# One attention loop instead of two: 20 steps that hold a differential and an MLA tile each, projections ahead of it, and norms computed on four columns

## The reference

```python
proj = rmsnorm(x, norm_mix) @ w_in       # 1920 columns: 15 chunks of 128
ua, cq, ckv, kr, qc, kc, vc, ud = split(proj)
ya = silu(layernorm(causal_dwconv31(glu(ua)))) @ pw + pw_b
yb = mla(rmsnorm(cq) @ w_uq, rmsnorm(ckv) @ w_ukv, rope)      # 4 heads, causal softmax
a0, a1 = softmax(q0 k0 + bias), softmax(q1 k1 + bias)         # 4 heads, two maps each
yc = rmsnorm((a0 - lam * a1) @ v)                             # "differential" attention
yd = ((windowed mean of ud) - ud) @ pool_w
x = x + concat(ya, yb, yc, yd) @ w_out
x = x + cross_attention(rmsnorm(x), rmsnorm(mem))   # its K and V: 16 chunks of mem @ wk, wv (256 tokens)
x = x + (silu(dwconv3(h @ up_g)) * dwconv3(h @ up_a)) @ down  # h = rmsnorm(x), width 2816
```

## Time and profile before

| what | value |
|---|---|
| three runs | 1738.75, 1740.1, 1740.25 us; median 1740.1 |
| the profiled execution | 1737.64 us, its span 1735.8 us |
| busy share of the span | PE 93%, PEld 71%, DVE 65%, ACT 40%, POOL 15% |
| mean granted TensorE clock | 0.975 of full speed |
| attention loop of layer 0, with the first two output chunks | 201.2 to 382.4 us |
| the same stretch of layer 1 | from 999.1 us on |

### The profile page before, as it was taken

How to read it: one execution, slowest core, us unless ns; L and a number is a source line. 1 busy time by engine, 2 the same in 40 slices (tenths; PEclk the granted TensorE clock), 3 DMA queues, 4 the chain that set the end, 5 groups by cost and what they waited for, 6 DMA issues and landing times. The chain is left out here.

```text
span 1735.8 us, 21837 instructions
## 1 busy us (share of the span) xinstructions
PE 1613.4 (93%) x7472; PEld 1239.5 (71%) x7472; DVE 1125.3 (65%) x1600; ACT 700.0 (40%) x1074; POOL 263.1 (15%) x176
## 2 busy tenths in 40 slices
PE   6889889889999999999988998899999999999996
PEld 3467576568767888888876666557867788888874
DVE  8968896664446764764765978665444674575575
ACT  3232355663344432432443244764243442342343
POOL 5513142112011000000020513212102000000002
PEclk9989999899999999999998999999999999999998
DMA  3142123223212333333224212322312232322323
GB/s 136 47 155 86 49 86 104 79 74 97 73 37 85 97 97 98 97 97 96 93 79 143 82 42 85 104 90 73 97 37 73 85 97 97 97 97 90 96 81 109
DMA packets 46205, 153.37 MB, mean 88 GB/s; under 512 B 5808, under 2 KB 6064, under 8 KB 45232
## 3 DMA queue, kind: packets, MB, share of 16 engines
q1 hardware_dynamic: 46128, 152.34, 27.5%
HBM read 144.97 MB, written 7.34 MB: 88 GB/s over the span
## 5 line engine op out<-in xcount | busy, mean ns | idle before, releaser
L688 ACT ACTIVATE wh<-raw 128x1024 fp32r<-128x1024 f32 x246 | 260.3, 1059 | 647.9 <-PE psum L1238 647.8
L1236 PE MATMUL psum<-a_hi,wh 128*128 128x512 f32 x1072 | 426.2, 398 | 12.2 <-DVE wl L927 11.8
L1237 PE MATMUL psum<-a_lo,wh 128*128 128x512 f32 x1072 | 420.4, 392 | 0.0
L1238 PE MATMUL psum<-a_hi,wl 128*128 128x512 f32 x1072 | 420.2, 392 | 0.0
L927 DVE TENSOR_TENSOR wl<-raw,wh 128x1024 fp32r<-128x1024 f32 x210 | 261.5, 1246 | 140.9 <-ACT wh L688 140.9
L1236 PE MATMUL psum<-b_hi,wh 128*128 128x512 f32 x608 | 240.2, 395 | 10.5 <-DVE wl L927 6.1
L1236 PEld LDWEIGHTS psum<-a_hi,wh 128*128 128x128 f32 x1072 | 203.1, 189 | 62.7 <-DVE wl L927 16.6
L1238 PE MATMUL psum<-b_hi,wl 128*128 128x512 f32 x608 | 236.7, 389 | 0.0
L1237 PE MATMUL psum<-b_lo,wh 128*128 128x512 f32 x608 | 236.7, 389 | 0.0
L1237 PEld LDWEIGHTS psum<-a_lo,wh 128*128 128x128 f32 x1072 | 203.2, 190 | 45.0 <-issue 2.9
L1238 PEld LDWEIGHTS psum<-a_hi,wl 128*128 128x128 f32 x1072 | 203.2, 190 | 42.7
(11 more groups left out here) (213 smaller groups left out, 2139.5 us busy)
## 6 DMA issues: line engine op xcount, KB each, us to landing
raw<-in_w_main SPq DMA_DIRECT2D x106, 512.0 KB, 3.5
raw<-in_w_up SPq DMA_DIRECT2D x88, 512.0 KB, 3.5
raw<-in_w_down SPq DMA_DIRECT2D x32, 512.0 KB, 3.5
raw<-in_w_last SPq DMA_DIRECT2D x16, 384.0 KB, 2.9
bias_scratch<-stage SPq DMA_DIRECT2D x64, 64.0 KB, 1.6
bias<-bias_scratch SPq DMA_DIRECT2D x16, 256.0 KB, 4.4
raw<-in_w_first SPq DMA_DIRECT2D x6, 512.0 KB, 3.5
sw<-in_small SPq DMA_DIRECT2D x2, 1152.0 KB, 6.7
```

Of the source, the lines that this page charges most:

```text
L688: act.activation(wh[:, b].rearrange("p k m -> p (k m)")[:, 0:width], raw[:, b, 0:width], ACT.Copy).then_inc(w_hi, 1)
L1236: pe.matmul(out_ap, wh[:, b, k, :], his[:, k, :], start=(begin and i == 0), stop=False)
L1237: pe.matmul(out_ap, wh[:, b, k, :], los[:, k, :], start=False, stop=False)
L1238: last = pe.matmul(out_ap, wl[:, b, k, :], his[:, k, :], start=False, stop=(end and i == len(tiles) - 1))
```

## The change

**Order.** Chunks 12, 13 and 14 run ahead of the loop (with the high parts of 14, 15 and 16, the exponential of lambda and the high part of the memory ahead of it on ACT as well). The loop then has 20 steps. Step t holds differential tile t (both maps), MLA tile t-1, the transposes of differential tile t-2 and MLA tile t-3, a pair of differential (even t) or MLA tiles (odd t) times values, and memory chunk t+14, whose 24 matmuls are cut in two halves of 12 with the MLA work in between. Both kinds of transposes use one bank, `TR[0]`; bank 5 becomes a third bank for the small products. The bias tiles move to other buffers and other places in SP's queue. Of the convolution's taps 43 are done ahead of the loop and 19 in steps 0 to 5 (before: 32 and 30). POOL does the high part too (`upper`) for chunks 25 to 32.

**Thin norms.** `sums_of` uses the squares as stationary operand and one column of ones as moving one, so that the sum of 128 tokens lands as one column: four columns for 512 tokens (eight for `sub`, with two heads each). ACT's root and DVE's reciprocal work on 128x4 or 128x8. `row_of` brings the result back onto all partitions: it multiplies a column, repeated as stationary operand, by the identity. For the three model norms ACT copies that row to SBUF (`row_of` on ACT). The others are read from PSUM. The last norm of the kernel (L1484 to L1502) stays as it was.

```diff
+STEPS = 20
+VX_AT = {11: 0, 13: 1, 15: 2, 17: 3}
+BIAS_AFTER = {N_WK: (0, 1, 2, 3), 19: (4,), 20: (5,), 21: (6,), 22: (7,), 23: (8,), ...
+POOL_HI = range(25, N_OUT + 2)
...
@@ sync
-                    loads_of(N_WK, 10, w_main, src_base=N_WK)
...
-                        if u in (0, 1):
-                            sp.wait_ge(acc_done, 2)
-                        elif u == 2:
-                            sp.wait_ge(v_full, V_AT["stat_kv"] + 1)
-                        elif u == 3:
-                            sp.wait_ge(g_dve, N_WK)
+                        if u == 0:
+                            sp.wait_ge(v_full, V_AT["stat_kv"] + 1)
+                        elif u == 1:
+                            sp.wait_ge(m_lo, KT)
+                        elif u == 2:
+                            sp.wait_ge(g_dve, N_WK)
+                        elif u == 3:
+                            sp.wait_ge(m_lo, KT)
...
-                    for n in range(25, 35):
+                    for n in range(N_WK, 35):
                         load(n, n % 2, w_main[layer, n])
                         for u in BIAS_AFTER.get(n, ()):
                             load_bias(u)
@@ gpsimd
+                    def upper(n):
+                        pool.wait_ge(w_load[n % 2], loads(n, n % 2))
+                        pool.wait_ge(g_full, n - 1)
+                        pool.wait_ge(w_hi, n)
+                        pool.tensor_copy(wh[:, n % 2].rearrange("p k m -> p (k m)"), raw[:, n % 2, :]).then_inc(w_hi, 1)
...
@@ scalar
+                    def roots(name, eps, scale, cols=4):
+                        act.activation(thin[:, ROOTS.index(name), 0:cols], v_wait(name)[:, 0:cols], ACT.Sqrt, bias=eps,
+                                       scale=scale).then_inc(root, 1)
+                    def row_of(name):
+                        act.activation(rbc[:], v_wait(f"{name}_row"), ACT.Copy).then_inc(v_act, 1)
...
                     for t in range(STEPS):
+                        if 2 <= t < 18:
+                            evict_pt("diff", t - 2)
                         if t < 16:
+                            exp_map("diff", t, 0)
+                            exp_map("diff", t, 1)
+                        if 3 <= t < 19:
+                            evict_pt("mla", t - 3)
+                        if 1 <= t < 17:
+                            exp_map("mla", t - 1, 0)
...
                         if n is not None:
+                            if n + 2 not in POOL_HI:
+                                hi(n + 2)
                             act.wait_ge(g_full, n + 1)
@@ vector
+                    def inverse(name, cols=4):
+                        r = ROOTS.index(name)
+                        dve.wait_ge(root, r + 1)
+                        dve.reciprocal(thin[:, r, 0:cols], thin[:, r, 0:cols]).then_inc(root_inv, 1)
...
                     for t in range(STEPS):
                         if t < 16:
...
                             for m in range(2):
+                                negatives("diff", t, m, dring[:, (2 * t + m) % 8, :], bias[t % 4], C_DIFF)
                         if 1 <= t < 17:
...
+                            inverse_sums("diff", u, slice(k, k + 2))
                             step(dve.tensor_scalar(e1, e1, rec[:, k + 1:k + 2], lam[:, 4:5], ALU.mult, ALU.mult))
                             dve.scalar_tensor_tensor(e0, e0, rec[:, k:k + 1], e1, ALU.mult,
+                                                     ALU.add).then_inc(p_ready, 1)
...
+                            negatives("mla", u, 0, ering[:, u % RING, :], mask[:, tile_at(u)[1], :], C_MLA)
+                        if 2 <= t < 18:
...
+                            dve.tensor_scalar(e, e, rec[:, u:u + 1], None, ALU.mult).then_inc(scaled_in, 1)
+                        if t < 6:
+                            convolve(4 if t == 0 else 3)
@@ tensor
+                    def sums_of(name, *pairs):
+                        ps, w = bank(name), pairs[0][1].shape[1]
+                        for j in range(4):
+                            for i, (src, one) in enumerate(pairs):
+                                last = pe.matmul(ps[:, w * j:w * j + w], src[:, P * j:P * j + P], one, start=(i == 0),
+                                                 stop=(i == len(pairs) - 1))
+                        last.then_inc(v_full, 1)
+                    def row_of(name, w=1):
+                        r = ROOTS.index(name)
+                        ps = bank(f"{name}_row")
+                        pe.wait_ge(root_inv, r + 1)
+                        for j in range(4):
+                            for i in range(w):
+                                inv = thin[:, r, w * j + i:w * j + i + 1].broadcast_to([P, P // w])
+                                last = pe.matmul(ps[P // w * i:P // w * (i + 1), P * j:P * j + P], inv, ident, ...)
+                        last.then_inc(v_full, 1)
...
                     for t in range(STEPS):
                         if t < 16:
+                            diff_scores(t)
+                        if t >= 4 and t % 2 == 0:
+                            weighted_pair("diff", t // 2 - 2)
+                        if 2 <= t < 18:
+                            turn("diff", t - 2)
+                        n = chunk_at(t)
+                        if n is not None:
+                            gemm(n, n % 2, memh, meml, M, ..., tiles=range(4), ready=ready, end=False)
+                        if 1 <= t < 17:
+                            mla_scores(t - 1)
+                        if t >= 5 and t % 2 == 1:
+                            weighted_pair("mla", t // 2 - 2)
+                        if 3 <= t < 19:
+                            turn("mla", t - 3)
...
                         if n is not None:
+                            gemm(n, n % 2, memh, meml, M, tiles=range(4, KT), ready=ready, begin=False)
```

More of the change, by code:

```diff
@@ L705, in _ @@
                     hi(1)
-                    act.activation(rtmp[:], v_wait("stat_mix"), ACT.Sqrt, bias=c("eps6"), scale=1.0 / D).then_inc(root, 1)
+                    roots("stat_mix", c("eps6"), 1.0 / D)
+                    row_of("stat_mix")
                     hi(2)
@@ L1329, in weighted_pair @@
[L1329 removed]
+                                                 ptr[:, 2 * int(kind == "diff") + place, kb, :], start=(kb == 0),
+                                                 stop=(kb == 3))
+                        last.then_inc(pv_done[kind] if qb < 3 else v_full, 1)
                     def y_ready(k):
@@ L1418, in norm_sum @@
                         pe.wait_ge(ss_in, n)
-                        product(name, (ones, ssum[:]))
+                        sums_of(name, (ssum, one))
                     gemm(N_WQ, 1, a_hi, a_lo, free="wq", ready=lambda i: pe.wait_ge(x_lo, i + 1))
                     norm_sum("stat_xa", KT)
-                    gemm(N_WQ + 1, 0, a_hi, a_lo, free="wq")
+                    gemm(N_WQ + 1, 0, a_hi, a_lo, free="wq", tiles=range(4), end=False)
+                    row_of("stat_xa")
+                    gemm(N_WQ + 1, 0, a_hi, a_lo, tiles=range(4, KT), begin=False)
                     gemms(N_WQ, KT, a_hi, a_lo, S, "wq", lead=2)
```

585 lines of the change are left out of this document (301 added, 284 removed).

## The result

The changed kernel takes 1715.3 us (median of four runs, 1713.1 to 1722.4) against 1740.2 (1738.8 to 1741.5) of the kernel before: ratio 0.9867, 95% interval 0.9841 to 0.9894. By the medians that is 24.9 us less; 28 were forecast, and 1715.3 lies in the range of 1684 to 1738.

A forecast was written before the change was run, and what follows sets the result against it. Bound by PE's own work plus hand-offs where its queue holds only the next link. Loop 141.9 + 5.6 + 17.2 + 3.5 + 1.7 = 169.9 against 181.2, 2.6 saved outside, 13.9 a layer: 1740.1 - 28 = 1712 us, range 1684 to 1738.

The forecast's parts named there:

- stalls, PE idle: Loop: stalls of PE at the start, in steps 1 to 17 and at the end, 17.2 us a layer together.
- small gaps and drain: Loop: small gaps remaining at the hand-offs cost 3.5 us a layer, against 9 before.
- half clock: Loop: one short stretch at half clock after the start's gap, 1.7 us.
- Start and steps 1 to 5: Loop's beginning: late load of chunk 16 5.5 us, DVE slowed by POOL's low parts 6.0, half clock 1.7.
- Tables of ACT (1.0) and POOL's copies (1.5): Loop: ACT's table changes in steps 8 to 13, 1.0 us; POOL's copies slowing DVE in steps 9 to 17, 1.5.
- Tail: Loop's end: 1.4 us idle for the last differential tile, 1.8 for chunk 33's low part, 3.2 together.
- Thin norms, 0.09 a record: Loop's norms on PE: 0.09 us a record, 0.06 if half-wide; 5.6 us, 2.2 more than the fat products.
- Outside the loop: Each layer: 2.2 us saved at the latents, 0.6 lost at stat_xa, 1.6 saved and 0.6 lost before feed-forward; net 2.6 saved.
- 1 (no charges): Loop: DVE isn't late, the start costs 2 us, one-column records 0.05; 1691 us in all; chance 0.20.
- 2 (POOL holds DVE): Loop: POOL stops DVE's taps and scalings for its whole 2.4 us, not 1.6; 1728 us in all; chance 0.10.
- 3 (single transpose bank): Loop: PE waits at MLA transposes for ACT's eviction, 2 us in 13 steps; 1764 us in all; chance 0.13.
- 4 (all gain eaten): Loop: PE's idle time moves and stays, 14 us a layer more than charged; 1740 us in all; chance 0.07.

The follow-up runs named there:

- control: The changed kernel run again unaltered, as yardstick beside the follow-up runs: 1715.9 us, 0.9864 of the kernel before; its profiled execution took 1714.88 us.
- e9: Changed kernel with three convolution taps moved from ahead of the memory's low parts to step 6: 1712.7 us, 0.9837 of the kernel before.
- e4: Changed kernel with 18 of the 19 convolution taps of steps 0 to 5 left out in each layer: 1705.4 us, 0.9804 of the kernel before.
- e8: e6 with the loop's taps spread over steps 0 to 7 and the layer norm's mean and variance a step later: 1700.5 us, 0.9776 of before.
- e3: Kernel before with the thin norms alone, order of loop, chunks and taps unchanged: 1743.4 us, 1.0022 of the kernel before.
- e6: Changed kernel with bias tiles 1 to 3 loaded behind chunk 17 and three taps moved to step 6: 1711.0 us, again 1710.9 us.
- e2: Changed kernel with each memory chunk run whole in the place of its first half: 1721.0 us, 0.9890 of the kernel before.
- e1: Changed kernel with bias tiles 1 to 3 loaded behind chunk 17's load instead of ahead of chunk 16's: 1717.9 us, 0.9877 of the kernel before.

## Why the prediction was right, and where it was off

**The loop, 169.9 forecast; 170.7, 170.8, 171.1 and 175.3 measured.** The sum came out, but its terms miss by more than it does, and cancel. That is luck. The control's layer 0, in the prediction's own terms (idle is length minus busy; the clock's term is half of the time at 0.50; the gaps are what is left over the forecast's 147.5):

| term | forecast | control |
|---|---|---|
| pieces and thin norms | 147.5 | taken as forecast |
| stalls, PE idle | 17.2 | 9.7 |
| small gaps and drain | 3.5 | 8.4 |
| half clock | 1.7 | 5.1 |
| sum | 169.9 | 170.7 |

The small gaps did not shrink from 9 to 3.5: by the same sum they were 7.4 before. Every bare step costs 6.8 to 7.0, not 6.6. The clock falls for 10.2 us of the loop, not for one short stretch of 3.4. And a part of the charged stalls didn't come. Place by place:

- Start and steps 1 to 5, 5.5, 6.0 and 1.7 charged, 13.2 together: from the end of chunk 14 to step 6 the pieces are 32.4, and 47.5 and 47.6 were measured in the control, 52.1 and 47.9 after. That is 15.1 and more over. The load landed in 6.3 (median of two; 6 taken). The step that failed is the claim that DVE empties chunk 14 2.3 us after PE's end. It ended that at 223.99 (the row of 223.30 above), 4.4 after PE's end, because POOL's first low part falls on the four taps ahead. PE therefore waits first for DVE, 2.7 in every layer, which the prediction didn't have, and then only 1.3 to 2.3 for `vc`, where it had one gap of 4. This second chain was not seen; e9 shows that it is the one that counts.
- Steps 3 to 6 alone take 4.8 and 4.7 over e4's 19.7 in the control, 7.0 and 4.7 after. That DVE's load is the cause is right, and e4 and e8 show it; what the prediction lacked is that in the control a third of it is clock. "About 8 in steps 2 to 5" fits only as a mean: single steps are 5.4 to 11.5.
- Tables of ACT (1.0) and POOL's copies (1.5): steps 6 to 15 have no idle time of PE. Nothing came of either, and no run shows a price for them. These steps still take 69.4 where the pieces give 65.7; the 3.7 are the gaps.
- Tail, 3.2 charged: 1.8 idle (the low part of chunk 33, the same row in the control as in e8), no other wait.
- Thin norms, 0.09 a record: 0.10, next.

Of the signs it named, the loop near 170, the waits at the MLA score, the missing wait for chunk 11 and the absence of waits for `ptr` came. PE's idle time near 12 to 15 did not (9.7 to 10.1, in one layer 13.2), nor steps of 6.6 from step 6 on, and one layer has the long stretch at half clock that was to be gone.

**The thin norms.** The records in the timeline of PE after: sums of `stat_q` (16) and `stat_kv` (8), the next chunk, and the rows (16):

```profile
163.64 2.45 PE L1347 MATMUL psum<-cst,sqx 128*128 128x1 f32 x16
166.03 1.05 PE L1347 MATMUL psum<-cst,ssum 128*128 128x1 f32 x8
166.94 0.47 PE L1306 MATMUL psum<-a_hi,wh 128*128 128x512 f32 x1
...
174.11 1.95 PE L1359 MATMUL psum<-cst,thin 128*128 128x128 f32 x16
```

Start to start 0.15 (2.39 / 16), 0.11 (0.91 / 8), and for `stat_ffn` 0.10, as for the 16 sums and 8 row records of `ln_var` in the control's loop; near the forecast's 0.09, far from the upper 0.43. The chunk after them takes 7.17 (174.11 - 166.94) instead of 5.44: the granted clock falls in it. The table of stretches after:

```profile
166.00:168.00 2.00, 2.00 (x13) 1.77 (x14) 1.12 (x4) 0.79 (x3) 1.85 (x3) 0.97 0.13 16
168.00:170.00 2.00, 2.00 (x6) 1.59 (x5) 1.93 (x3) 0.00 (x0) 1.92 (x2) 0.50 0.62 246
```

PE had no idle time there; what it did before the fall is the 24 records with one moving column. The kernel before, with two fat products in that place, has 1.00 throughout in both layers; all thirteen traces of kernels with thin norms show the fall in both, in the last eight of these records or within 1 us behind them; one of them is e3's, whose order is the old one. That it is these records that bring it is argued, not shown: behind the 16 of `ln_var` in the control's loop the clock stays at 1.00. The Trainium skill, "TensorE: Matmul & The Clock Gate", section "LDWEIGHTS (loading the stationary operand)", gives a weight load as its columns over 1.2 ns. By that, an estimate, 128 columns take 0.107. The best rows agree, 0.10; the 0.15 of the row of 16 doesn't.

**Outside the loop, -2.6 a layer forecast; +0.6 and -1.0 after, -1.0 and -1.6 in the control (from a layer's first chunk to the next layer's or the end, less the loop).** Up projection: -1.0 forecast, -3.1 measured, 89.00 above with no idle time and clock 1.00 against this row of before, from its first chunk on:

```profile
540.40:632.50 92.10, 89.92 (x388) 73.56 (x387) 66.56 (x86) 40.66 (x51) 1.29 (x1) 0.98 0.30 91
```

The 2.2 wait went whole, and with it the 3.4 us at half clock behind it, which the prediction had not priced. WQ: +0.6 forecast, +0.5 measured. Input projections: -2.2 forecast, and in the four layers 0.1 less to 0.9 more measured. The wait for chunk 11 went as said, but the records (0.7 more), the rows (1.7 and 0.8) and the half clock (1.7) took it. At the turn of the layer the gap before the first sum, "issue" in the waits, grew from 8.3 to 8.5, 8.9 and 10.3 in three traces; why stays open.

**The rivals.** 1 (no charges): no, the start and steps 1 to 5 cost what was charged and more. 2 (POOL holds DVE): the mechanism is right, the price isn't. POOL, then DVE, in step 2 of the kernel after:

```profile
240.66 2.40 POOL L676 TENSOR_TENSOR wl<-raw,wh 128x1024 fp32r<-128x1024 f32 x1 [6.19 <-ACT wh L714]
```

```profile
240.71 0.69 DVE L1088 CUSTOM_DVE_ANT_0 dring<-psum,rbc 128x512 f32<-128x512 f32 x1 [1.53 <-PE psum L1414]
...
241.32 0.69 DVE L1088 CUSTOM_DVE_ANT_0 dring<-psum,rbc 128x512 f32<-128x512 f32 x1
...
242.13 1.21 DVE L1137 TENSOR_SCALAR dring<-dring,rec,lam 128x512 f32<-128x512 f32 x1
```

The minima, with one input in PSUM, run at their 0.69 beside POOL; the scaling that follows ends at 243.34, 0.28 after POOL. A tap that meets POOL takes 2.0 more (e8), and four with one collision 5.12 against 3.11. So a meeting costs up to 2.1 of POOL's 2.4 (5.34 against 3.26), not 1.6, but the minima take part of it where they stand in front, and after step 5 DVE has room. Nor is the price the DVE instruction's size: in e6's second trace the small one behind the memory's low parts, 0.21 after (at 223.90), started 0.29 behind POOL's 219.24 and ended at 221.59, 0.01 after POOL:

```profile
219.53 2.06 DVE L1081 SCALAR_TENSOR_TENSOR lam<-lam,vec 128x1 f32<-128x1 f32 x1
```

 The Trainium skill, "SBUF — State Buffer", section "Who interferes with whom", has both halves: with at most one input in SBUF, and outside the two-port modes, a DVE instruction doesn't contend with GpSimd; with two it does, and so does one in a two-port mode. The trace agrees for the minima, the taps and this small one. The scaling reads one tile from SBUF and still took 1.21 beside POOL, against 0.55 alone in later steps; whether it ran in a two-port mode no run here shows. 3 (single transpose bank): no wait for `ptr` in the loop, not even in e2 (0.3). 4 (all gain eaten): no.

## What to carry to other kernels

Behind the wait that could be seen here stood a second chain of nearly the same length: look for one ahead of removing the first (e1 gave nothing, three taps moved on another engine 3 to 5 us). Where a second engine is as full as the bound one, look at which of its instructions are running when the engine that it collides with starts: where a third tap of 0.77 met POOL, leaving it out of the step gave back 2.8 of DVE. Price a wait of PE with the half clock behind it: 3.1 became 4.8 here. Read a right sum term by term: this one was right by three misses. Price a thin operation by its weight loads (0.10 a record here), and look at the clock behind it.

## What the hardware showed unexpectedly

- The clock fell to 0.50 with PE never idle, behind 24 matmuls with one moving column each (in the last eight of them or within 1 us behind, in thirteen traces and both layers), and the chunk behind them took 1.7 us longer.
- The changed kernel took 1712.2 to 1722.4 us in its twelve runs, e8 1699.7 to 1701.6. Its three traces differ by up to 4.5 us in one layer, all of it ahead of step 6: in whether taps and POOL's low parts meet, and in how long PE is at half clock. Whether slack there makes a kernel steadier isn't shown: the control's own four runs lie within 1.2 us, e8's five within 1.9.
- The loop's length is PE's idle time, plus half of its time at 0.50, plus 154.5 to 157.4 us, in each of the 24 loops of the twelve traces with the new order (162.5 to 175.3 us long). Most of what the variants differ by in the loop is in the first two terms.
- DVE's eight low parts of the memory took 3.26 us alone and 5.34 beside one POOL subtraction of 2.35, while its minima, which read PSUM, lost nothing beside one.
